# Eight of the sixteen modulation dot products move from VectorE to GpSimd and ScalarE, and VectorE's norm comes after its own eight

## The reference, cut to what matters

```
cs  = silu(c)                                  # one row of 1024
mod = cs @ w_ada + b_ada                       # 6 x 1024 outputs
shift1, scale1, gate1, shift2, scale2, gate2 = split(mod, 6)
h    = rms_norm(x, norm1_g) * (1 + scale1) + shift1
proj = h @ w_in                                # everything below needs h
```

## Time and profile before

| what | value |
|---|---|
| median of 3 runs | 1761.96 us (1761.9 to 1764.45) |
| the profiled execution: time | 1763.66 us |
| its span | 1761.8 us |
| mean granted TensorE clock | 0.926 of full |
| busy share of the span | PE 85%, DVE 50%, ACT 29%, POOL 17% |

### The profile page before, as it was taken

The page is one execution under the profiler, slowest core; times in us unless marked ns, Lnnn a source line. Parts: engine busy times, 40 slices in busy tenths (PEclk is TensorE's granted clock), DMA queues, the critical chain, the costliest instruction groups (busy, mean ns, idle before and its releaser), DMA issues.

```text
span 1761.8 us, 24728 instructions
## 1 busy us (share of the span) xinstructions
PE 1491.7 (85%) x9560; PEld 1198.4 (68%) x9560; DVE 880.6 (50%) x2241; ACT 510.7 (29%) x1284; POOL 295.8 (17%) x260
## 2 busy tenths in 40 slices
PE   2999998689888989887886799989589888888887
PEld 1888887679888888887786468868445444444444
DVE  5687756877777777777743224622622111111112
ACT  2152212344444444444432210120222222221221
POOL 0000000444444454454441000000000000000000
PEclk7999999899999999999898799959689999999999
DMA  9453884999999999999999344923159999999994
GB/s 393 191 195 139 341 339 167 396 420 421 421 414 419 414 421 420 419 412 421 420 421 425 138 165 179 418 92 144 48 244 429 428 429 429 429 429 429 429 429 210
DMA packets 60561, 595.63 MB, mean 338 GB/s; under 512 B 6848, under 2 KB 7232, under 8 KB 7616
## 3 DMA queue, kind: packets, MB, share of 16 engines
q1 hardware_dynamic: 23616, 326.11, 44.9%
q0 software_dynamic: 36864, 268.45, 36.8%
HBM read 593.48 MB, written 1.05 MB: 337 GB/s over the span
## 4 chain that ended last, share of the span: by engine, by line
PE 50%; DMA 34%; DVE 12%; ACT 2%; issue 2%; SPq 0%; POOL 0%; DVEq 0%; POOLq 0%; ACTq 0%
PE bank L577 20%; DMA weight_slabs<-in_w_moe 19%; PE bank L770 13%; DMA gathered_rows<-in_expert_uv,work 10%; PE bank L892 4%; DMA weight_slabs<-in_expert_uv,work 4%; PE bank L799 2%; PE bank L731 2%; DVE weight_slabs L1550 1%; PE bank L868 1%; DVE gathered_rows L1550 1%; PE bank L596 1%; DVE work L1497 1%; DVE work L1495 1%; DVE work L1531 1%
## 5 line engine op out<-in xcount | busy, mean ns | idle before, releaser
L770 PE MATMUL bank<-work,weight_slabs 128*128 128x128 f32 x2048 | 278.4, 300 | 82.2 <-ACT work L1096 82.2
L770 PEld LDWEIGHTS bank<-work,weight_slabs 128*128 128x128 f32 x2048 | 270.7, 214 | 93.7 <-ACT work L1096 91.0
L770 PE MATMUL bank<-work,gathered_rows 128*128 128x128 f32 x2048 | 251.1, 279 | 29.2 <-ACT work L1096 29.1
L770 PEld LDWEIGHTS bank<-work,gathered_rows 128*128 128x128 f32 x2048 | 243.2, 194 | 38.9 <-ACT work L1096 36.3
L577 PE MATMUL bank<-hT,weight_slabs 128*128 128x256 f32 x992 | 218.7, 383 | 20.3 <-ACT hT L959 20.3
L1550 DVE CUSTOM_DVE_ANT_0 gathered_rows<-gathered_rows,work 128x1024 f32<-128x1024 f32 x128 | 157.0, 1229 | 150.4 <-DMA gathered_rows<-in_expert_uv,work 150.4
L577 PEld LDWEIGHTS bank<-hT,weight_slabs 128*128 128x128 f32 x992 | 191.0, 193 | 46.9 <-issue 21.2
L1157 POOL DMA_INDIRECT gathered_rows<-in_expert_uv,work x128 | 148.1, 1157 | 440.5 <-DVE work L1537 307.8
L892 PE MATMUL bank<-weight_slabs,work 128*32 128x512 f32 x1024 | 132.3, 663 | 61.6 <-DMA weight_slabs<-in_w_moe 60.3
L1157 POOL DMA_INDIRECT weight_slabs<-in_expert_uv,work x128 | 147.5, 1153 | 205.9 <-PE bank L770 201.4
L1550 DVE CUSTOM_DVE_ANT_0 weight_slabs<-weight_slabs,work 128x1024 f32<-128x1024 f32 x128 | 151.3, 1222 | 52.6 <-DMA weight_slabs<-in_expert_uv,work 52.6
(11 more groups left out here) (317 smaller groups left out, 1605.4 us busy)
## 6 DMA issues: line engine op xcount, KB each, us to landing
weight_slabs<-in_w_moe SPq DMA_DIRECT2D x96, 2048.0 KB, 20.6
weight_slabs<-in_slabs SPq DMA_DIRECT2D x55, 2048.0 KB, 11.5
weight_slabs<-in_slabs SPq DMA_DIRECT2D x2, 1024.0 KB, 10.3
gathered_rows<-in_expert_uv,work POOLq DMA_INDIRECT x128, 13.1
weight_slabs<-in_expert_uv,work POOLq DMA_INDIRECT x128, 11.9
weight_slabs<-in_slabs SPq DMA_DIRECT2D x1, 1664.0 KB, 28.3
weight_slabs<-in_slabs SPq DMA_DIRECT2D x1, 1280.0 KB, 17.7
silu_c_rows<-in_c_row SPq DMA_DIRECT2D x2, 512.0 KB, 4.9
```

What stands on the lines that cost most here:

```text
L770: last = nc.tensor.matmul(ps[c // 2][:, (c % 2) * T + t * P:(c % 2) * T + (t + 1) * P], row_at[k][:, D + c * P:D + (c + 1) * P], diag[:, k ...
```

## The change

- The third and the fourth slab (`ada2`, `ada3`) leave `slab_dots` and `DOTTED`. GpSimd multiplies each quarter of them by `crow` in place (four `tensor_tensor` of 128x1024 for each slab), and raises `shared_products` after each.
- ScalarE, between its square root and `modulated(0)`, copies each quarter onto itself with a running sum (`accum_out`) into the column of `mod`, and raises `shared_dots`.
- VectorE does `ada0` and `ada1` first, then `stream_norm(0, ...)`, and then waits for all eight `shared_dots` before `mod_bias`.
- SP waits on `shared_dots` before it loads into the slots of `ada2` and `ada3`.

```
--- before.py
+++ after.py
@@ program
-    DOTTED = [f"ada{i}" for i in range(12)] + [f"bda{i}" for i in range(12)]
+    SHARED = ["ada2", "ada3"]
+    DOTTED = [f"ada{i}" for i in (0, 1, *range(4, 12))] + [f"bda{i}" for i in range(12)]
@@
+    shared_products, shared_dots = sem("shared_products_ready"), sem("shared_dots_done")
@@ block.sync
+            if slab_before[n] in SHARED:
+                sp.wait_ge(shared_dots, 4 * SHARED.index(slab_before[n]) + 4)
             if slab_before[n] in DOTTED:
                 sp.wait_ge(dots_done, DOTTED.index(slab_before[n]) + 1)
@@ block.scalar
         root(1, T)
+        for i, name in enumerate(SHARED):
+            for q in range(4):
+                w = slabs[:, SLOT[SLAB_AT[name]], q * D:(q + 1) * D]
+                act.wait_ge(shared_products, 4 * i + q + 1)
+                A(w, w, ACT.Copy, accum_out=mod[:, 0, 8 + 4 * i + q:9 + 4 * i + q]).then_inc(shared_dots, 1)
         modulated(0)
@@ block.gpsimd
+        pool.wait_ge(silu_ready, 1)
+        for name in SHARED:
+            n = SLAB_AT[name]
+            pool.wait_ge(slab_loaded[SLOT[n]], slab_value[n])
+            for q in range(4):
+                w = slabs[:, SLOT[n], q * D:(q + 1) * D]
+                nc.gpsimd.tensor_tensor(w, w, crow[:, :], ALU.mult).then_inc(shared_products, 1)
         for m in range(NPAIR):
@@ block.vector
         slab_dots("ada0")
         dve.wait_ge(consts_in, 32)
         dve.wait_ge(x_in, 16)
+        slab_dots("ada1")
         stream_norm(0, "ss1", "n1")
-        for i in range(1, 4):
-            slab_dots(f"ada{i}")
+        dve.wait_ge(shared_dots, 8)
         mod_bias(0, 0)
```

## The result

The changed kernel takes 1769.62 us (median of 6 runs, 1768.28 to 1771.91) against 1763.23 us for the kernel before in the same comparison (6 runs, 1761.9 to 1764.67). The ratio is 1.0037, 95% interval 1.0024 to 1.005: slower by 0.24 to 0.5%. The forecast was 1766.5, range 1762 to 1773, slower.

A forecast was written before the change was run, and what follows sets the result against it. TensorE waits through a 41 us lead-in set by VectorE's chain to `mod_bias`. Eight GpSimd products (24.65 + 8 x 2.3) plus 1.24 move it from 39.75 to 44.3; 1761.96 + 4.5 = 1766.5 us, range 1762 to 1773.

The forecast's parts named there:

- What bounds the start, and what was removed: Lead-in: VectorE's chain up to `mod_bias` at 39.75 keeps TensorE waiting; 8 dots, 9.4 us, leave that path.
- The price of a product, p = 2.3: GpSimd, lead-in: each 128x1024 product takes 2.3 us, twice VectorE's 1.14; an estimate that counts eightfold.
- ScalarE: Lead-in: eight copies with a sum, 1.16 us each, keep pace; only the last is on the path, 1.24 us with semaphores.
- The lead-in's sum: Start of `mod_bias`: 24.65 + 8 x 2.3 plus 1.24 gives 44.3 against 39.75, +4.5 us.
- contention: First two GpSimd products beside VectorE's norm: GpSimd held for 0 to 1.6 us; 0 taken as likeliest.
- Blocked or held at the start: Rival, lead-in: p 2.3 to 2.67 with up to 1.6 and 1.28 us on top; 1769 to 1772.4; 15%.
- the forecast's own 1765 to 1769: Total time in the main case, p from 2.1 to 2.5 with little contention; 56%.
- cost of a first instruction: GpSimd's start in the lead-in: bounded by nothing below and a table load's 1.28 us above.
- the contention rule: Skill's rule: two-input VectorE instructions and GpSimd instructions reading SBUF contend, the later waits; sum between +4.5 and +6.1 us.
- VectorE's norm: Lead-in, after `ada1`: runs 24.45 to 28.9; waiting there costs nothing, having 15 us of room.
- SP's queue and GpSimd's later work: Later loads: `in_lg0` has 45 us of cover, GpSimd's queue is empty until 307.8 us; both at nothing.
- The shift is passed on in full: From lead-in to kernel end: loads and gathers move with TensorE, so the whole +4.5 us reaches the total.

The follow-up runs named there:

- e3: Changed kernel with GpSimd's eight multiplications replaced by signals alone, ScalarE summing raw weights (modulation false, only the lead-in read); bias at 33.81.
- e12: As e10, with three quarters on GpSimd and VectorE's ada0 to ada3 dots reading the silu row from PSUM; 1760.45 us against 1763.15, ratio 0.9981.
- e7: Changed kernel with GpSimd multiplying each quarter by constant 1.0 instead of the silu row (only the lead-in read); bias at 47.94.
- e5: Changed kernel with GpSimd and ScalarE doing ada2 alone and VectorE doing ada3 after the norm; bias at 39.87, ratio 1.0002 against the kernel before.
- e6: Changed kernel with the norm ahead of ada1, as before, so VectorE's dots lie beside GpSimd's products; bias at 48.86, ratio 1.0053.
- e10: As e11, with the first norm's refining steps reading one operand from PSUM, none two tensors from SBUF; bias at 36.31, ratio 0.9986.
- e11: Kernel before with e1's order, GpSimd and ScalarE doing two of the four quarters of ada2; bias at 38.02, ratio 1.0.
- e4: Kernel before with four more VectorE multiplications of 128x1024 ahead of the bias, nothing on GpSimd; bias at 44.27, ratio 1.0032.
- e1: Kernel before with only the order changed, ada1 ahead of the norm, VectorE doing all dots; bias at 38.30, ratio 0.9995.
- e8: Kernel before, VectorE only, ordered ada0, ada1, variance, ada2, inverse root, ada3; bias at 38.23, ratio 0.9995.
- e9: As e8, with the four 128x256 refining steps on GpSimd beside VectorE's ada3; bias at 37.96, ratio 0.9992.

## Why the prediction was right, step by step

**What bounds the start, and what was removed:** right. In e3 the bias comes at 33.81 as soon as the products are gone.

**The price of a product, p = 2.3:** right in size, for a reason that no run bears out; the closeness is in part luck. Undisturbed products follow each other every 2.32 us (e12, 6.96 for three). I had built it as two operands fetched one after the other, each at VectorE's rate. By that, one operand should take 1.0 to 1.3 us, and in e7 it took 2.75. That was another instruction, though, so e7 doesn't say what sets the 2.32 of the product; that stays open. The nearest row was the scan's 2.67. The Trainium skill's figure ("GPSIMD Engine Reference", section 3.1), halved to 2.25, is borne out by the 2.32. That this engine is the wrong one for elementwise work (section 4.1) is borne out for this change, whose products set the end of the lead-in, but e12 gains with three of them.

**ScalarE:** right. 1.16 us after the last product, and 1.27 with semaphores, against 1.24.

**The lead-in's sum:** 24.67 + 19.1 + 1.27 = 45.04 against 44.3 forecast, +5.3 us instead of +4.5. The term that was undersized is contention, which I took at 0: four VectorE steps held GpSimd by 19.09 - 8 x 2.32 = 0.5 us. The rest is mostly 0.02 us in each product. Contention at the start was also the mechanism of the rival "Blocked or held at the start", and the measured 1769.62 lies in its band of 1769 to 1772.4, outside the forecast's own 1765 to 1769. By its terms the rival came true only in small part: 0.5 us of contention out of up to 1.6, and no cost of a first instruction to be seen (the first product starts at 24.67); 1.3 us of the 1769.62 are the higher base below. The prediction also says that the contention rule puts the time in that band; by its own +4.5 to +6.1 us the rule gives 1766.5 to 1768.1, below it.

**VectorE's norm:** wrong, without a price here. I expected it to end at 28.9 and it ended at 36.94; the stretched steps cost 9.59 - 1.58 = 8.0 us. I had written that it costs nothing if VectorE waits because of 15 us of room; 8.1 of them are left. In e5, where VectorE has work behind the norm, the same steps eat the whole gain. The rule that I quoted (the Trainium skill, "SBUF — State Buffer", section "Who interferes with whom") agrees with e6, e10, e11 and e12: steps and dots with two tensors in SBUF wait for the running product, those with one of them in PSUM don't. It does not agree with e7, where GpSimd's instruction also reads SBUF and two steps with two tensors there did not wait for its end (1.14 and 0.43 us); there the measurement decides, and the rule is shown only for GpSimd's product of two tensors. The same section names the kind of the single-operand step that took 2.33 us, `tensor_scalar`, among the instructions that can use both port pairs. It took 0.29 us alone from SBUF and 0.42 from PSUM in e10. The reciprocal, also with one operand, kept its 1.75.

**SP's queue and GpSimd's later work:** costs nothing, as said; TensorE's 62 us behind the lead-in are unchanged.

**The shift is passed on in full:** right for the delays, within what can be told, and open for the gains. Taking the start of the bias from the median time leaves between 1723.4 and 1725.6 us for the kernel before, the change and the ten of these experiments that compute the whole modulation (all but e3 and e7), over bias times from 35.03 to 48.86. The two that compute something else, and so may route the tokens otherwise, leave 1723.1 (e3) and 1728.4 (e7), with one execution each. e4 shows it without GpSimd. The scatter of 1 us on either side hides gains under 2 us, which is why e1, e8, e9 and e11 can't be told from before. It is not even on both sides: in its four comparisons the kernel before leaves 1723.4 to 1724.3 us, and nine of the eleven others leave more than it does in the same comparison. For e10, e11 and e12 it is 1725.3 to 1725.6 against 1723.4. So about 2 us of their earlier start are not in the times. A part may be the 39.75 itself, which moves by 0.5 us (e4). A larger part shows up between the bias and the first gather, 268.5 us before and 269.8 to 270.3 in these three, with a granted clock of 0.98 and 0.97. Each of these is one profile, and what makes the difference stays open.

**The total:** 3.1 us over the forecast; against the kernel before in the same comparison 6.4 us, where 4.5 was forecast. 0.8 is the lead-in, 1.3 is that the kernel before itself came out at 1763.23 in this comparison and not at 1761.96; the last 1.0 is within the scatter and has no shown cause. The reason for the loss is settled; this remainder is not.

## What to carry to other kernels

Before work is given to GpSimd beside VectorE, count the SBUF tensors that VectorE's instructions read meanwhile: with two of them VectorE and GpSimd's products of two tensors take turns by whole instructions, and a helper of half the speed makes the pair slower than VectorE alone (e5, e6; another instruction of GpSimd, e7, didn't hold VectorE so). Putting one operand in PSUM (a row that is used again and again is the natural one) made them run side by side, and then the helper's share has to be cut so that it ends when VectorE does: eight products lost 0.37%, three, with the operands in PSUM, won 0.19%. PSUM alone would not have saved the eight: by the rows, 24.67 + 8 x 2.32 + 1.27 = 44.5 is an estimate of the bias even without contention. An edit in a lead-in is priced by when the next stage can start: there is a gain only if the helper's own chain, from the landing of its data to its last result, ends before the work that stays with VectorE. Here its products alone were 18.6 us, and they took 9.4 us of work away.

## What the runs showed of the hardware that was not expected

- A GpSimd multiplication by a constant (one tensor operand, 128x1024) took 2.75 us, longer than the product of two tensors at 2.32.
- The exclusion is unequal for short and long steps: a VectorE step of 0.43 us with two tensors in SBUF waits for the whole product and then holds GpSimd by 0.18 us, one of 0.29 us with constants by 0.04; a dot of 1.22 us holds it by 0.97 us (e6).
- Beside a GpSimd multiplication by a constant, VectorE's steps with two tensors in SBUF were not held to its end (e7).
- The same instructions of the last expert took 3.64 or 6.60 us in two executions of one kernel, at a granted clock of 1.00 or 0.71 (a mean over a stretch that lies partly at each of the two levels, 2.4 and 1.2 GHz). TensorE had waited 2.9 us for a load ahead of either. From the start of the bias to the first gather it was 268.5 us before and 272.0 in e8, with a granted clock of 0.98 and 0.96 from the first product on.
